# Six small expert slots in three pairs, longer runs in the weight loads, an earlier ring of four and shorter lists

## The reference

```python
glog = (t @ w_rg + b_rg)                      # 4 groups
gval, gidx = lax.top_k(softmax(glog), 1)
elog = (t @ w_re + b_re).reshape(-1, 4, 4)
elog_sel = take_along_axis(elog, gidx[:, :, None], axis=1)[:, 0]
evals, eidx = lax.top_k(elog_sel, 2)          # 2 experts of the group
ew = softmax(evals) * gval
combine = sum(one_hot(gidx * 4 + eidx, 16) * ew[..., None], axis=1)
for e in range(16):
    he = silu(t @ w_gate[e]) * (t @ w_up[e])  # 1024 -> 512
    y = y + combine[:, e:e + 1] * (he @ w_down[e])   # 512 -> 1024
```

## Time and profile before

| | us |
|---|---|
| median of 3 runs | 2129.55 |
| lowest and highest | 2128.95, 2136.04 |
| profiled execution: its own time | 2135.79 |
| profiled execution: span of the trace | 2133.9 |
| PE busy | 2057.7 (96%) |
| PEld busy | 1612.1 (76%) |
| DVE busy | 1269.4 (59%) |
| ACT busy | 991.0 (46%) |
| POOL busy | 146.0 (7%) |

### The profile page before, as it was taken

One profiled execution on the slowest core, in us unless ns is written; L12 is line 12 of the kernel. 1 busy time (PEld: TensorE's weight loads), 2 busy tenths in 40 slices (PEclk: granted clock), 3 DMA queues, 4 the chain that ended last, 5 costly groups with the idle time before them and its releaser, 6 DMA issues.

```text
span 2133.9 us, 28078 instructions
## 1 busy us (share of the span) xinstructions
PE 2057.7 (96%) x10671; PEld 1612.1 (76%) x10671; DVE 1269.4 (59%) x2200; ACT 991.0 (46%) x1642; POOL 146.0 (7%) x246
## 2 busy tenths in 40 slices
PE   8999999999999999989999999999999998999996
PEld 7877778888888877768888888887788797545562
DVE  5575766576846266656766856747744566344563
ACT  4445545445534355545554454533742252244452
POOL 0000020000011000001000002102000001111110
PEclk9999999999999999989999999999999998899998
DMA  6235334642532324313426353443335316979997
GB/s 210 71 104 170 98 122 145 197 157 71 198 109 88 120 94 146 102 40 119 158 70 207 91 186 119 134 130 122 100 109 180 119 63 213 375 257 359 370 367 269
DMA packets 219005, 339.19 MB, mean 159 GB/s; under 512 B 15712, under 2 KB 103024, under 8 KB 218864
## 3 DMA queue, kind: packets, MB, share of 16 engines
q1 hardware_dynamic: 214672, 327.09, 46.2%
q0 software_dynamic: 4192, 10.23, 2.0%
HBM read 307.91 MB, written 31.72 MB: 159 GB/s over the span
## 4 chain that ended last, share of the span: by engine, by line
PE 79%; DVE 6%; DMA 6%; ACT 3%; POOL 2%; issue 2%; SPq 1%; DVEq 0%; ACTq 0%; POOLq 0%
PE ps L181 74%; PE ps L184 5%; DMA RAW<-in_w_down_dram 2%; POOL SM L216 1%; SPq L221 1%; DVE WL L196 1%; DMA ONDP<-qkd 1%; ACT ST L192 1%; DVE X L206 1%; POOL SM L213 1%; DMA ed<-ST 1%; ACT WH L192 0%; DMA NQ<-qqd 0%; DMA KTr<-ktd 0%; DVE BR L196 0%
## 5 line engine op out<-in xcount | busy, mean ns | idle before, releaser
L196 DVE TENSOR_TENSOR WL<-RAW,WH 128x1024 fp32r<-128x1024 f32 x388 | 467.8, 1222 | 258.7 <-ACT WH L192 254.7
L192 ACT ACTIVATE WH<-RAW 128x1024 fp32r<-128x1024 f32 x388 | 404.2, 1055 | 321.7 <-PE ps L181 175.7
L181 PE MATMUL ps<-XH,WH 128*128 128x512 f32 (+1 forms) x880 | 324.0, 368 | 2.9 <-DVE WL L196 2.9
L181 PE MATMUL ps<-XL,WH 128*128 128x512 f32 (+1 forms) x880 | 321.4, 365 | 0.0
L181 PE MATMUL ps<-XH,WL 128*128 128x512 f32 (+1 forms) x880 | 321.0, 365 | 0.0
L181 PE MATMUL ps<-WH,XH 128*128 128x512 f32 (+1 forms) x736 | 296.8, 403 | 2.3 <-ACT ST L192 2.3
L181 PE MATMUL ps<-WH,HR 128*128 128x512 f32 x928 | 289.3, 390 | 0.0
L181 PE MATMUL ps<-WH,XL 128*128 128x512 f32 (+1 forms) x736 | 284.9, 387 | 0.0
L181 PE MATMUL ps<-WL,XH 128*128 128x512 f32 (+1 forms) x736 | 284.4, 386 | 0.0
L181 PEld LDWEIGHTS ps<-WH,HR 128*128 128x128 f32 x928 | 174.2, 188 | 36.0
L181 PEld LDWEIGHTS ps<-XH,WH 128*128 128x128 f32 x880 | 168.6, 192 | 29.0 <-DVE WL L196 3.1
(11 more groups left out here) (357 smaller groups left out, 2928.0 us busy)
## 6 DMA issues: line engine op xcount, KB each, us to landing
RAW<-in_ffn_w_dram SPq DMA_DIRECT2D x164, 512.0 KB, 4.5
RAW<-in_w_gate_dram SPq DMA_DIRECT2D x62, 512.0 KB, 11.7
RAW<-in_w_up_dram SPq DMA_DIRECT2D x61, 512.0 KB, 12.3
RAW<-in_w_down_dram SPq DMA_DIRECT2D x57, 512.0 KB, 12.0
RAW<-in_w_in_dram SPq DMA_DIRECT2D x30, 512.0 KB
RAW<-in_ev_w_in_dram SPq DMA_DIRECT2D x20, 512.0 KB
RAW<-in_ple_w_gate_dram SPq DMA_DIRECT2D x16, 512.0 KB
RAW<-in_od_w_in_dram SPq DMA_DIRECT2D x32, 256.0 KB
```

Source lines behind the costliest of these rows:

```text
L181: return self.go(ns).matmul(o, lhsT=l, rhs=x, start=st, stop=sp)
L192: return self.go(0.83 * n + 55.0 + (130.0 if bias is not None else 0.0) + (100.0 if acc is not None else 0.0)).activation(o, i, f, scale=s ...
L196: return self.go(1.04 * n + 68.0).tensor_tensor(o, a, b, op)
```

## The change

1. Slots (2, 3), (4, 5) and (7, 8) form pairs. One gather of 128 rows fetches both lists (rows 64 to 127 are the second slot's), 128-row turns of XG and ES serve both, and they share one EF and one EG. The products with weights stay apart for each slot. `GROUPS` has a new order.
2. `tile_k` reads the experts' weights with pieces of 4096 bytes: a partition takes two neighbouring rows of gate or up (512 columns), or one whole row of down (1024 columns). Partition p starts at row 8p (4p for down), so that the partitions' pieces are 16 KB apart. A down tile now is one k with both halves of the columns, and `turned` picks the columns to match.
3. WH and WL have four buffers from the products with `w_cq` on (`MARKS["few"]`), and slots 24 to 31 may be filled as soon as their last tenant is used up. They stand right behind the first three in the order of slots.
4. The lists of 64 rows are made by one product each with the identity, from the lists of 128 rows; the two parts of the weight list are made side by side in 52 columns and added by VectorE. 72 products become 18.
5. Small slots' folds take banks of the ring S and not OP (except 16 and 17).

```diff
+    def tile_k(w, k, n):
+
+
+        if n == 512:
+            return w.rearrange("(p k) c -> p k c", k=8)[:, k:k + 2, :], "B"
+        return w.rearrange("(p k) (s c) -> p k s c", k=4, s=2)[:, k, :, :], "B"
+
...
-    GROUPS = ((0,), (1,), (15, 17), (2,), (14, 16), (3,), (13,), (4,), (12,), (5,), (11,), (6,), (10,), (9,), (7,), (8,))
...
+    GROUPS = ((0,), (1,), (15, 17), (2, 3), (14, 16), (4, 5), (13,), (12,), (6,), (11,), (10,), (9,), (7, 8))
     SLOTS = sum(GROUPS, ())
     LAST = SLOTS[-2:]
+
+    def steps(gr):
+        return [(i,) for i in gr] if small(gr[0]) else [gr]
+
+    def lead(i):
+        return i - 1 if i in (3, 5, 8) else i
+
+    def paired(i):
+        return lead(i) in (2, 4, 7)
+
+    LEADS = [i for i in SLOTS if lead(i) == i]
 
     def small(i):
         return i < 9 or i in (16, 17)
...
-                split = sum(w is not None for w in WAT[MARKS["moe"]:]) if "moe" in MARKS else None
+                split = sum(w is not None for w in WAT[MARKS["few"]:]) if "few" in MARKS else None
...
             for n, gr in enumerate(GROUPS):
-                yield from fan(gr)
+                for one in steps(gr):
+                    yield from fan(one)
                 if n:
-                    yield from fold(GROUPS[n - 1])
-            yield from fold(GROUPS[-1])
+                    for one in steps(GROUPS[n - 1]):
+                        yield from fold(one)
+            for one in steps(GROUPS[-1]):
+                yield from fold(one)
...
-        def weight(gr, name, k, n):
+        def weight(gr, name, k):
 
             i, use = gr[0], "both" if len(gr) > 1 else "whole" if small(gr[0]) else "split"
             if i < 2:
-                return tile(*tile_b(A[name][0, 15 - i], k, n), use)
-            return tile((name, k, n, 16 + i if i < 18 else i - 17), "B", use)
+                return tile(*tile_k(A[name][0, 15 - i], k, 1024 if name == "w_down_2" else 512), use)
...
-                        ex, o = pe.slot("ex", i)[1], pe.slot("fan", i)
+                        ex, o, n = pe.slot("ex", lead(i))[1], pe.slot("fan", i), 64 * (i - lead(i))
                         for g, (c, _, _) in enumerate(tiles):
-                            t = pe.mm(o[64 * g:64 * g + 64, :], ex[:, k, :], whole_tile(c)[:, k % 2, :], k == 0, k == 7, 445)
-                        keys = done(i, tiles[0][0]) + done(i, tiles[1][0]) + ([("fan", i), ("free", ("ex", i))] if k == 7 else [])
+                            p = 64 - 64 * g if paired(i) and i == lead(i) else 64 * g
+                            t = pe.mm(o[p:p + 64, :], ex[:, k, n:n + 64], whole_tile(c)[:, k % 2, :], k == 0, k == 7, 432)
+                        keys = done(i, tiles[0][0]) + done(i, tiles[1][0])
+                        if k == 7:
+                            keys += [("fan", i)] + ([("free", ("ex", lead(i)))] if i > lead(i) or not paired(i) else [])
                         if keys:
...
-                if k % 2 == 0:
-                    tiles = [weight(gr, "w_down_2", k, 512 * nh) for nh in range(2)]
...
+                c, wh, wl = weight(gr, "w_down_2", k)
...
                     if small(i):
-                        pe.wait_ge(*(yield [("eh", i), *[("raw", c) for c, _, _ in tiles],
-                                            OP.ask(("fold", i)) if k == 0 else None]))
...
+                        ring = OP if i in (16, 17) else S
+                        pe.wait_ge(*(yield [("eh", lead(i)), ("raw", c), ring.ask(("fold", i)) if k == 0 else None]))
+                        eh, o, n = pe.slot("eh", lead(i))[1], pe.slot("fold", i), 64 * (i - lead(i))
+                        for nh in range(2):
+                            t = pe.mm(o[64 * nh:64 * nh + 64, :], eh[:, k, n:n + 64], whole_tile(c)[:, nh, :], k == 0, k == 3, 432)
+                        keys += [("fold", i)] if k == 3 else []
                         if keys:
```

The lists, the wait of the turns, the gates of a pair, VectorE's copies, and the order of slots:

```diff
-            l3, r64 = RF[:, 128:336].rearrange("p (b t) -> p b t", b=8), R8[:, :, 0:64].bitcast(F32)
+            both = RF[:, 96:608].rearrange("p (s c) -> p s c", s=2)
             pe.wait_ge(*(yield [("r8", 0), ("r8", 1), ("ot3",), OP.ask(("place",))]))
             o = pe.slot("place")
             for b in range(8):
-                pe.mm(o[:, 0:26], R8[:, b, :], ot3[:, b, :], b == 0, b == 7, 60)
-            for h in range(2):
-                for b in range(8):
-                    t = pe.mm(o[64 * h:64 * h + 64, 32:58], r64[:, b, :], ot3[:, b, :].bitcast(F32), b == 0, b == 7, 60)
+                t = pe.mm(o[:, 0:26], R8[:, b, :], ot3[:, b, :], b == 0, b == 7, 112)
             t.then_inc(*pe.sig("pe_attn", ("place",)))
+            pe.wait_ge(*(yield [("pf",)]))
+            pe.mm(o[64:128, 32:50], ident[:, 0:64], RTV["pf"][:, 0:18], True, True, 224).then_inc(
+                *pe.sig("pe_attn", ("again",)))
             pe.wait_ge(*(yield [("l3",), OP.ask(("cw",))]))
             o = pe.slot("cw")
             for b in range(8):
-                pe.mm(o[:, 0:26], R8[:, b, :], ot3[:, b, :], b == 0, False, 60)
-                pe.mm(o[:, 0:26], R8[:, b, :], l3[:, b, :], False, b == 7, 60)
-            for h in range(2):
-                for b in range(8):
-                    pe.mm(o[64 * h:64 * h + 64, 32:58], r64[:, b, :], ot3[:, b, :].bitcast(F32), b == 0, False, 60)
-                    t = pe.mm(o[64 * h:64 * h + 64, 32:58], r64[:, b, :], l3[:, b, :].bitcast(F32), False, b == 7, 60)
+                t = pe.mm(o[:, 0:52], R8[:, b, :], both[:, :, 32 + 26 * b:58 + 26 * b], b == 0, b == 7, 112)
             t.then_inc(*pe.sig("pe_attn", ("cw",)))
+            pe.wait_ge(*(yield [("rw",)]))
+            pe.mm(o[64:128, 64:82], ident[:, 0:64], ROWW[:, 0:18], True, True, 224).then_inc(
+                *pe.sig("pe_attn", ("cwagain",)))
 
...
             for k0 in range(0, K, 4):
-                pe.wait_ge(*(yield [(name + "in", i), TP.ask((name + "T", i, k0))]))
+                pe.wait_ge(*(yield [(name + "in", i), (name + "in", i + 1) if name == "es" and paired(i) else None,
+                                    TP.ask((name + "T", i, k0))]))
...
+                    p = 0 if paired(i) and i == j else 64
+                    a.wait_ge(*(yield [("fan", i), ask, *after_cross]))
+                    a.act(a.slot("esin", j)[p:p + 64, :], a.slot("fan", i)[64 - p:128 - p, :], AF.Silu, 512).then_inc(
                         *a.sig("act_evac", ("sil", i)))
...
-            v.ts(pf, b[:, 0:26], 1000.0, None, ALU.add, None, 26).then_inc(*v.sig("dve_vec"))
-            v.ts(ps, b[:, 32:50], 1000.0, None, ALU.add, None, 18).then_inc(
-                *v.sig("dve_vec", d.new(), ("free", ("place",))))
+            v.ts(pf, b[:, 0:26], 1000.0, None, ALU.add, None, 26).then_inc(*v.sig("dve_vec", d.new(), ("pf",)))
             v.cp(IOTA[:, :], iota, 128).then_inc(*v.sig("dve_vec", ("iota",)))
+            v.wait_ge(*(yield [d.k]))
+            v.cp(ps[0:64, :], pf[0:64, 0:18], 18).then_inc(*v.sig("dve_vec"))
+            v.wait_ge(*(yield [("again",)]))
+            for i in (2, 4, 7):
+                v.cp(IDX[64:128, i:i + 1], b[64:128, 33 + i:34 + i], 1).then_inc(*v.sig("dve_vec", ("idx", "pairs")))
+            v.cp(ps[64:128, :], b[64:128, 32:50], 18).then_inc(*v.sig("dve_vec", d.new(), ("free", ("place",))))
```

The last changed places are the condition for slots 24 to 31 and their place in the line of slots:

```diff
         if slot > 23:
-            return after_cross
+            return [("wf", max(c for c in range(MARKS["few"]) if WAT[c] == 4 + slot % 4))]
...
-            line = sorted((0, 1, 2), key=lambda n: tenant[n][0:2]) + [9, 10, 11, 12, 3, 4, 5, 13, 14, 6, 7, 8, 16, *range(24, 32)]
+            line = sorted((0, 1, 2), key=lambda n: tenant[n][0:2]) + [
+                *range(24, 32), 9, 10, 11, 12, 3, 4, 5, 13, 14, 6, 7, 8, 16]
```

114 lines of the change are left out of this document (64 added, 50 removed), and 2 rows, old and new, of the table scored.

## The result

| | before | after |
|---|---|---|
| median of 5 runs, us | 2129.55 (2127.69 to 2136.04) | 2116.72 (2109.61 to 2121.43) |
| profiled execution, us | 2135.79 | 2121.43 |
| its span, us | 2133.9 | 2119.6 |
| granted clock | 0.981 | 0.982 |

The ratio is 0.9937 with a 95% interval of 0.9914 to 0.9959, so 9 to 18 us faster. On another chip, beside another 11 runs of before, it was 0.9918 (0.9893 to 0.9944), from 2131.90 to 2114.26 us. The forecast of 2106 was 10.7 too low, and 2116.72 lies within the range of 2093 to 2121.

A forecast was written before the change was run, and what follows sets the result against it. The prediction took the kernel's end as bound by TensorE, and in two places by weights it runs into. Terms summed to -23.3 us off the profiled 2135.79 (2112.5), less that run's 6.2 excess: 2106 us, range 2093 to 2121.

The forecast's parts named there:

- lists: Routing lists on TensorE: 100 fewer records save 8.0 us, two new waits cost 0.5; -7.5 us (-8.0 to -6).
- start: Start of the expert stage: gathers land in 5 us, so the first fan starts near 1812; -2.8 us (-3.8 to 0).
- waits of TensorE in the stage: Expert stage: longer pieces and earlier tiles end TensorE's waits for weights, 10.6 us in all; -10 us (-10.6 to -4).
- clock in the stage: Expert stage: two of four dips of TensorE's granted clock, 3.4 us each, go; -7 us (-12 to 0).
- pairs (turns): Small expert slots: 128-row turns replace two of 64, with fewer copies and gathers; -1 us (-2 to 0).
- cross attention: Stage before the experts: the early ring moves w_co's copies and subtractions into the softmax; +3 us (0 to 9).
- tail: End of kernel: fold 9's scatter and the loads of `sum` get less cover; +2 us (-0.8 to +9).
- Rival two: End of kernel: the `sum` loads become last, +9 us and not +2, giving 2113 us; chance 0.11.
- the signs: Included 20 list records taking some 1.7 us, and clock 1.00 in all windows but the first and last 20 us.
- Long pieces: Queue q1: 4096-byte pieces cost 0.933 of 2048-byte ones per MB, 1.50 us a tile for 1.60, 1.51 in the sum.
- rival four: Weight loads: pieces 16 KB apart cost more, deciding from 1.79 us a tile (193 ns a packet) on, so slower; chance 0.05.
- rival one: Cross attention stalls as w_co's halves come late: +9 us and not +3, 2112 us, or 2115 with a clock dip; chance 0.12.

The follow-up runs named there:

- no_pairs: The changed kernel without pairs, each small slot gathered, turned and copied by itself, groups in the old order: 2114.30 us, 0.9922.
- copies: Kernel of mid_both with ScalarE's copies of slot 11's down result moved into the middle of fan 9, slot 10's ahead of fold 9's conversions: 2106.85 us, 0.9884.
- tail: The changed kernel with ScalarE's copies for slot 10 ahead of the silus of slots 7 and 8, which take other EY buffers: 2113.15 us, 0.9941.
- short_runs: The changed kernel with the experts' weights in 2048-byte pieces as before, all else as changed: 2117.10 us, 0.9949.
- mid_both: Kernel of tail, with slot 9's ES turn behind fold 10, slot 11's copies before slot 9's silu, ring of four starting behind the w_cq products: 2107.72 us, 0.9889.
- before_again: The unchanged kernel from before the change, run and profiled once more: one run of 2130.21 us.
- late_short: The changed kernel with late ring and 2048-byte pieces as before; pairs, short lists and new group order stay: 2119.82 us, 0.9961.
- down_rows: Kernel of copies with each down tile taking 128 successive rows, its 4096-byte pieces 4 KB apart and not 16: 2104.47 us, 0.9887.

## Why the prediction was near, and where it was not

By the forecast's terms; measured is the mean of two profiles each of before and after, what lies ahead of 1685 us left out.

| term | forecast | measured |
|---|---|---|
| lists | -7.5 | -6.7 (9.3 to 2.6) |
| start | -2.8 | -2.1 |
| waits of TensorE in the stage | -10 | -5.1 (14.1 to 9.0) |
| clock in the stage | -7 | -6.3 (11.4 to 5.1) |
| pairs (turns) | -1 | -0.2 |
| cross attention | +3 | +6.5 (4.8, and 1.7 of clock) |
| tail | +2 | -0.2 behind the last SELF |
| rest of TensorE's work in the stage | none | -3.4 |
| sum | -23.3 | -17.4 |

The medians moved by 12.8 and 17.6 us, and the measured sum lies within the intervals of both (9 to 18 and 12 to 23 us). Part of it is luck: the waits gave half of their term and cross attention took twice its own, and 3.4 us of less work, for which the forecast had no term, made up for less than half of that.

- **Waits for weights.** "So weights stop being what it runs into" came out: 10.6 us of the earlier trace rows went to nothing. The term failed since it took only off. Of other waits there had been 3.2 us, and now there are 9.0: 3.5 and 1.6 for ES, 1.4 for a bank, 2.5 for EY. The 3.5 and the 1.4 come of the order of the groups with slot 9 and the pair (no_pairs has not got them), the last, for the most part, of the EY buffer. The forecast had asked what is late next only of the DMA. Its lead was also smaller than it said. It had the last tile there at 2067, 2078 with the 11 us that after is late at the stores; the tile landed at 2088.7, some 8 us before fold 8 took it. That fits with the weights being the bound again once the other waits were mended (copies).
- **The tail.** Rival two did not come about in after, by a margin of 0.95 us: the scatter took 6.2 us and the loads of `sum` 9.4 from the first issue to the last landing, where the forecast had 8.8 and 5 to 7. In tail it did: there the end waited for these loads.
- **The start.** The mechanism is as forecast, and stronger: the gathers took 3.2 us and not 5, and nothing waits for XG. The size is loose: of the 2.1 us measured 0.6 are clock, and before's own two profiles differ by 2.5 there.
- **The lists.** 20 records cost 2.6 us and not the 1.7 named as a sign: the 0.080 us of a record is a mean of 128-row ones at 0.125 and 64-row ones at 0.066, and those that stay are of the former. The two new waits, charged with 0.5, were not there.
- **The clock.** The dips behind the lists and at 1990 us went, as said; a new one stands behind the waits at slot 9 (2059 us), so the clock was not full in the middle of the stage, as the signs had it. In before each dip of 3.4 us lost is 6.8 us long.
- **Long pieces** were sized well where the queue is full (1.51 us a tile for 1.51), and rival four fell: 39.9 engine-us per MB with the pitch of 16 KB, 40.9 against 40.8 when only the pitch of the down tiles changes. A packet of 4096 bytes took 162 ns on average. (Rival four's 193 ns for 1.79 us a tile comes out as 199 with the 89.1% of the earlier trace rows.) By the Trainium skill, "DMA: Bandwidth & Descriptors", section "Why small descriptors are slow (HBM only)", the longer packets should have saved an estimated 2.2%. Between short_runs and after, 43.2 against 39.9 is 7.6%, so here the measurement decides. What the Trainium skill lists for rows in HBM at large powers of two apart (same page, section "Latency and other measured facts") starts at 512 KiB; no run here shows a loss at 16 KB.
- **Turns.** "Fan and fold matmuls stay as they are", and so they did, but the layout that the pieces ask for was not priced where it ends up: in the operand of the turns, 3.0 us. (Of the 0.2 us in the table, slot 1's turn, which moved ahead of the stage, is 0.7; without it the turns would have cost 0.5 more.)
- **Cross attention** was rival one in mechanism at half of its size: 4.8 us, of which 2.2 are idle time of TensorE in many small waits, none over 0.64. mid_both shows the cause, since 3.6 us went when two of the four conversions no longer waited.
- **The basis.** Taking the sum off the profiled execution and then going down by its 6.2 us of excess held: before_again shows that the terms repeat (stage 308.2 and 307.1).

What stays open: the 3.4 us of TensorE's work that are neither lists nor turns, and the 5.3 us of waits for weights that were gone in late_short too, were not traced further.

## What to carry to other kernels

When a change takes one engine's waits for data away, look next at the order of its queue: an instruction that stood harmlessly ahead while the data was late becomes the wait. Here three such places (a turn ahead of a fold, two copies behind conversions, a buffer picked by number) left 9.0 us of waits where 10.6 for the weights had gone, and when they were mended the weights, and at the very end the loads of `sum`, were the bound again. A layout chosen for the DMA must be priced at every engine that then reads with a stride.

## What the runs showed of the hardware

- Loading a TensorE operand of fp32 whose columns lie 4 or 8 apart took 212 and 193 ns (after), side by side 140 (short_runs; 139 in down_rows). Turns of 128 rows hid most of it (XG 279 against 275 ns a record, ES 303 in copies against 283 in down_rows), turns of 64 rows did not (277 and 293 against 228 and 232).
- From 1950 to 2070 us, with q1 full, 4096-byte pieces took 39.9 engine-us per MB (after) and 2048-byte pieces 43.2 (short_runs). A partition pitch of 16 KB or of 4 KB in the down tiles made no difference (40.9 in copies, 40.8 in down_rows, 1815 to 2040 us).
- The first gather took 8.2 us to land while SyncE was issuing weight loads (before, from 1803.52 us on) and 3.2 us when it issued none (after, from 1807.4 to 1819.2 us).
